# Gathering the first expert's tokens with the selection as the stationary operand

## The reference, cut to what matters

```python
def moe_swiglu(h, router, w1, w3, w2):
    logits = t @ router                       # t: 256 x 1024
    top_val, top_idx = lax.top_k(logits, 2)
    gates = softmax(top_val)
    # tokens of each expert are gathered in blocks, then for each block:
    #     y = (silu(xi @ w1[e]) * (xi @ w3[e])) @ w2[e]
    # w1, w3: 1024 x 3584, w2: 3584 x 1024 for each of 8 experts
    # and out[token] += y * gate
```

## Time and profile before

| | us |
|---|---|
| median of 3 runs | 1779.2 |
| lowest and highest | 1776.2 and 1781.97 |
| the profiled execution, its own time | 1776.49 |
| its span in the trace | 1774.6 |
| the gather on TensorE (L2348) | from 878.61, for 7.95 |
| item 0's first product (L2378) | 887.21 |

### The profile page before, as it was taken

How to read it: one execution, slowest core, us unless ns; L and a number is a source line. 1 busy time by engine, 2 the same in 40 slices (tenths; PEclk the granted TensorE clock), 3 DMA queues, 4 the chain that set the end, 5 groups by cost and what they waited for, 6 DMA issues and landing times.

```text
span 1774.6 us, 30337 instructions
## 1 busy us (share of the span) xinstructions
PE 1727.1 (97%) x13214; PEld 926.7 (52%) x13214; DVE 638.7 (36%) x1091; ACT 404.6 (23%) x796; POOL 202.2 (11%) x269
## 2 busy tenths in 40 slices
PE   7999989999999999999999999999999999999998
PEld 3787656878788888666833332333323233233433
DVE  2634586789855775362311001010110102001112
ACT  3523484422222223376100100001000010000010
POOL 1416332011101110433100000000000000000010
PEclk9999999999999999999999999999999999999999
DMA  9454500779664544133489999999999999999993
GB/s 357 145 189 170 151 1 3 258 264 322 206 221 143 190 137 168 48 131 118 157 331 418 416 393 419 396 414 417 388 419 398 410 417 391 418 403 407 417 421 161
DMA packets 136284, 498.40 MB, mean 281 GB/s; under 512 B 6849, under 2 KB 47425, under 8 KB 127969
## 3 DMA queue, kind: packets, MB, share of 16 engines
q1 hardware_dynamic: 132624, 489.58, 72.0%
q0 software_dynamic: 1920, 5.77, 1.1%
q10 hardware_dynamic: 1616, 1.22, 0.2%
HBM read 474.13 MB, written 22.41 MB: 280 GB/s over the span
## 4 chain that ended last, share of the span: by engine, by line
PE 84%; DMA 5%; DVE 5%; ACT 2%; POOL 2%; issue 1%; SPq 0%; ACTq 0%; DVEq 0%; POOLq 0%
PE ps L2378 31%; PE ps L2394 10%; PE ps L2197 6%; PE ps L2199 6%; PE ps L2198 6%; PE ps L2401 5%; DMA ring_up<-in_moe_w 4%; PE ps L2048 2%; PE ps L2069 2%; PE ps L1989 2%; PE ps L1990 2%; PE ps L1991 2%; PE ps L2143 2%; PE ps L2088 1%; PE ps L2112 1%; DMA ring<-in_ffn_w_up 1%
## 5 line engine op out<-in xcount | busy, mean ns | idle before, releaser
L2378 PE MATMUL ps<-ring_up,xg 128*32 128x448 f32 x3840 | 366.7, 539 | 3.4 <-DMA ring_up<-in_moe_w 3.4
L2378 PEld LDWEIGHTS ps<-ring_up,xg 128*32 128x32 f32 x3840 | 118.8, 110 | 246.0 <-issue 240.1
L2378 PE MATMUL ps<-ring,xg 128*32 128x448 f32 x2304 | 223.5, 542 | 0.7 <-DVE xg L1900 0.7
L1862 DVE TENSOR_TENSOR hid<-hid,ps 128x448 f32<-128x448 f32 x48 | 26.9, 617 | 531.8 <-PE ps L2378 531.8
L2378 PEld LDWEIGHTS ps<-ring,xg 128*32 128x32 f32 x2304 | 71.6, 110 | 147.3 <-issue 145.5
L2197 PE MATMUL ps<-hTh,fsa 128*128 128x512 f32 x328 | 128.7, 392 | 3.7 <-DVE fsb L1642 3.4
L2199 PE MATMUL ps<-hTl,fsa 128*128 128x512 f32 x328 | 128.1, 391 | 0.0
L2394 PE MATMUL ps<-ring_up,hidT 128*32 128x512 f32 x1024 | 121.3, 592 | 1.1 <-DMA ring_up<-in_moe_w 1.1
L1198 ACT ACTIVATE fsa<-ring 128x1024 fp32r<-128x1024 f32 (+2 forms) x73 | 68.8, 943 | 226.0 <-PE ps L2199 220.0
L1310 ACT ACTIVATE ytok<-ps 32x512 f32<-32x512 f32 x32 | 18.8, 589 | 412.5 <-PE ps L2401 412.3
L1361 DVE SCALAR_TENSOR_TENSOR scr<-ring,scond,scr 128x512 f32<-128x512 f32 x140 | 110.8, 826 | 1.1
(11 more groups left out here) (327 smaller groups left out, 2517.0 us busy)
## 6 DMA issues: line engine op xcount, KB each, us to landing
ring_up<-in_moe_w SPq DMA_DIRECT2D x80, 1792.0 KB, 19.8
ring<-in_moe_w SPq DMA_DIRECT2D x48, 1792.0 KB, 19.5
ring<-in_ada_w SPq DMA_DIRECT2D x24, 2048.0 KB, 8.3
ring<-in_moe_w SPq DMA_DIRECT2D x24, 2048.0 KB, 24.5
ring_up<-in_moe_w SPq DMA_DIRECT2D x24, 2048.0 KB, 24.2
ring_up<-in_moe_w SPq DMA_DIRECT2D x16, 1024.0 KB, 22.9
ring<-in_ev_w_in SPq DMA_DIRECT2D x6, 2048.0 KB, 10.5
ring<-in_ffn_w_gate SPq DMA_DIRECT2D x11, 1024.0 KB, 6.9
```

Of the source, the lines that this page charges most:

```text
L2378: ins = pe.matmul(ps[3 * z + t][32 * q:32 * q + 32, 0:FC], xg[:, k, 32 * t:32 * t + 32], w[:, c, FC * q:FC * (q + 1)], start=(k == 0), sto ...
```

## The change

In `gather_first` the operands change places. `sel` becomes stationary, 32 of the 96 token columns at a time, and `htok` moves, 256 neighbouring features at a time. The four quarters of the 1024 features go to the four column quarters of the array, so token j of quarter q ends at partition 32q + j. That is 3 token groups x 2 token tiles x 4 quarters = 24 products of 32 x 256. Each token group has its own PSUM bank (4, 5, 3), and `m_gat` counts three. The result isn't in `xg`'s layout: each 32 x 32 block has to be turned. VectorE does that with one transpose for each token group, from PSUM straight into `xg`, reading features with a step of 8. The transposes stand on VectorE directly behind the step that gives the number of items, and ahead of its register load. ScalarE's copy and VectorE's copy go away.

```diff
@@ ScalarE
-            act.wait_ge(m_gat, 1)
-            act.activation(xg[:, 0:4, :], v3(ps[4][:, 0:4 * CAP], CAP), ACT.Copy).then_inc(m_x, 1)
@@ VectorE
             dve.tensor_scalar(nit[:, 0:1], col[5][:, 1:2], float(NE - 1), None, ALU.add).then_inc(items_rd, 1)
+            for t in range(GT):
+                dve.wait_ge(m_gat, t + 1)
+                ins = dve.transpose(xg[:, :, 32 * t:32 * t + 32],
+                                    ps[(4, 5, 3)[t]][:, 0:256].rearrange("p (i c) -> p c i", c=KT))
+            ins.then_inc(m_x, 2)
             dve.wait_ge(items_rd, 1)
...
-            dve.wait_ge(m_gat, 2)
-            dve.tensor_copy(xg[:, 4:8, :], v3(ps[5][:, 0:4 * CAP], CAP)).then_inc(m_x, 1)
@@ TensorE, gather_first
-                for hh in range(2):
-                    for q in range(4):
-                        for t in range(2):
-                            rows = htok[:, t, :].rearrange("p (i c) -> p c i", c=KT)
-                            ins = pe.matmul(ps[4 + hh][:, q * CAP:(q + 1) * CAP], rows[:, 4 * hh + q, :],
-                                            sel[:, t, :], start=(t == 0), stop=(t == 1))
+                for t in range(GT):
+                    for h in range(2):
+                        for q in range(4):
+                            ins = pe.matmul(ps[(4, 5, 3)[t]][32 * q:32 * q + 32, 0:256],
+                                            sel[:, h, 32 * t:32 * t + 32], htok[:, h, 256 * q:256 * q + 256],
+                                            start=(h == 0), stop=(h == 1))
                     ins.then_inc(m_gat, 1)
```

## The result

The changed kernel takes 1769.1 us, the median of 17 runs (1764.4 to 1776.5), against 1777.0 for the kernel before in 17 runs alongside (1771.2 to 1784.9). The ratio is 0.995, with a 95% interval from 0.9938 to 0.9962, so the gain is between 6.8 and 11.0 us. The three runs of before that were shown had a median of 1779.2. With 17 runs it is 1777.0, so the starting point was 2.2 us too high and the gain about 3 us too small.

A forecast was written before the change was run, and what follows sets the result against it. TensorE was taken to pace most of the expert stage and the DMA stream its end. TensorE's gain of 4.5 + 1.35 = 5.8 us, capped at 5.0, gave 1779.2 - 5.0 = 1774.2 us, range 1769.5 to 1779.

The forecast's parts named there:

- the starting point: Time of the kernel before, from which the gain was subtracted: 1779.2 us, the median of three runs.
- the DMA stream: Weight transfers in the expert stage: can win only their idle time, 5.0 us, which caps TensorE's 5.8 us gain.
- the turning: Three VectorE transposes behind the gather, 0.66 us each, set its end; the first product comes 4.5 us earlier.
- the clock: Gather and start of item 0: the clock no longer falls to half, which gains 1.35 us in item 0.
- What bounds the kernel: Expert stage: TensorE sets the pace for most of it, the DMA stream at the end; 3.4 us of weight waits.
- The gather: Ahead of item 0: 48 pairs of 256 columns replace 32 pairs in 7.95 us, taking 2.62 us plus 0.16 tail.
- The 0.8 us of added late waits: Items 6 and 7: 0.8 us of TensorE's gain comes back as additional waiting for weights.
- (b): Rival, end of the expert stage: TensorE sets the end, so the whole 5.8 us count, 1773.4 us; chance 0.18.
- (a): Rival, gather and item 0: the clock falls all the same, gain 1.8 us, 1777.4, or 3 to 4.5; chance 0.20.
- (c): Rival, gather: the quarters' weight loads aren't hidden, 1778 us, or 1785.7 fully serial; chance 0.04 without and 0.03 with loss.

The follow-up runs named there:

- e3: The kernel before with the two 1024 KB units of each item loaded only to a quarter: 1770.8 us, ratio 0.9954.
- e5: The changed kernel with six more keep-busy TensorE products between the gather and item 0: 1777.0 us, ratio 0.999.
- e6: The changed kernel with six VectorE products ahead of the last transpose, so that TensorE idles: 1778.2 us, ratio 1.0003.
- e4: The changed kernel with the two 1024 KB units of each item loaded only to a quarter: 1765.4 us, ratio 0.9927.
- e7: The changed kernel with the gather products reordered so that four records in a row go to the same quarter: 1769.4 us, ratio 0.9948.
- e1: The kernel before, unchanged, with a second trace: 1778.5 us, ratio 1.0004.
- e10: The kernel before, unchanged, with a third trace: 1774.4 us, one run.

## Why the prediction was wrong

One step failed, the cap that the DMA stream was to put on the gain. The other mechanisms were the right ones, but two of their terms were too small: the turning and the clock. All three misses are in the gain and to the same side: 0.8 us by the cap, 0.65 by the turning and 0.85 by the clock. The starting point was off besides.

- **What bounds the kernel**: right. TensorE paces the expert stage until the weight stream has used up its lead, and e3 puts a price on the rest, 7 us in place of the 3.4 of the waits that I read. Those were the waits of L2378 alone; L2394 waited 1.3 us more for weights in the same trace.
- **The gather**: 2.80 us measured, 2.78 forecast. Scaling the item's product from 448 to 256 columns held within 1%.
- **The turning**: mis-sized. I took 0.66 us a transpose; two take 0.77 back to back and one alone 0.45. The nearest row by its step was the wrong guide; the floor from the transpose without a step (0.36) was close. With 0.66 VectorE sets the end. With 0.4 it waits for the last token group, and only one transpose lies behind the gather. The first product comes 5.1 us earlier, not 4.5.
- **The clock**: right in kind. It stays at 1.00, and e5 against e6 shows that what TensorE does before the item decides it. Its worth was read from the one trace at hand, 1.35 us. The four traces with the old gather lose 1.3 to 2.7, in the mean 2.3.
- **The DMA stream**: this step failed. I let it cap the gain at 5.0 us by adding up idle time from the DMA share. The bytes say 6.5 in the first pair of traces and 7.4 in the mean of three: after the gap a stretch with a share of 0.86 moved 276 GB/s, where item 1 with a share of 1.01 moved 408, and 0.86 of that would be some 350. Share is not rate. The stream did follow the first release of a slot, 6.36 us sooner against the gather's start, so it takes nothing from TensorE's gain. The 0.8 us of added late waits didn't come: late waits are 2.1 to 2.8 us in the three traces of the changed kernel and 2.7 to 6.2 in the three of the one before.
- **Rivals**: the time came out nearest to (b), with 5.8 to 6.7 us of gain, but not by its reason. TensorE does not set the end alone, as e3 and e4 show; the weight stream simply starts as much earlier as TensorE does. (a) was wrong (item 0 takes 108.2 us in all six traces with the early start) and (c) was wrong (e7).
- **The starting point**: three runs stood for a distribution with a spread of 14 us. Their median was 2.2 us high. From 1777.0 the same gain gives 1772.0, with a range of 1767.3 to 1776.8 around it, and the measured time lies in that. But the gain would have been as much too small.

The sum as the traces have it: 5.16 us of start (8.61 to 3.45) and 2.2 of clock (item 0 from a mean of 110.4 in three traces of before to 108.2) are 7.3 us, against 7.9 by the medians and an interval from 6.8 to 11.0. The clock on record for every run supports the second term: it is 6.0 us less clock time lost. Some 4 of these lie between the fall of the clock and item 0's first product, and cost nothing, since the old gather took 7.95 to 7.97 us however much of it ran at half clock. By this estimate some 2 us are left for item 0. What is left, 0.6 us by the medians and up to 1.6 by the ratio's middle, is within the scatter of the late waits. Whether the change shortens these by a microsecond or two can't be told from eleven traces, and stays open.

## What to carry to other kernels

Where a small product is bound by loading 128-column operands that have a step, swap the operands and put four quarters side by side: here 7.95 us became 2.80, and the layout was repaired by three transposes of 0.4 us of which only the last was exposed. When a stage is paced by a stream that is released by the first use of a buffer, a saving ahead of it moves the stream too; judge that by the bytes moved up to a given point, not by the share of busy DMA engines. And price a clock dip from several executions: it is worth different amounts in each, and time won at one dip can be lost at another. The mean granted clock of every run says what one trace can't.

## What the runs showed of the hardware

- A VectorE transpose of 128 x 256 from PSUM, read with a step of 8, took 0.39 us back to back (0.77 for two) and 0.45 alone; one of 128 x 384 from SBUF with the same step takes 0.866. The shorter form costs less than half, which neither proportion (0.58) nor the difference of two rows (0.74) told.
- Four records in a row to one column quarter ran as fast as neighbours in different quarters (2.85 against 2.80 us for 48).
- The old gather took the same time at both clocks: 7.95 us where its first 1.03 us were at full clock, 7.97 in e1 and e10, where all but the first 0.2 to 0.3 us were at half. That is 0.25 us a pair. Weight loads fill nearly all of it, as the first row below shows; the next two rows, from just before the gather, are pairs with 128 columns of weights that lie side by side and 8 that move, at 0.11 us a pair (0.22 from the start of one row to the next). So the loading of weights with a step of 8 sets the old gather's pace, and not the columns that move; that the step is what makes it slow is likely from these rows, but no run changed the step alone.

```profile
878.61 7.71 PEld L2348 LDWEIGHTS ps<-sel,etab 128*128 128x128 f32 x32 [1.47 <-DVE sel L1812]
```

```profile
876.42 0.37 PE L2337 MATMUL ps<-etab,ones 128*128 128x8 f32 x2
876.65 0.37 PE L2338 MATMUL ps<-etab,ones 128*128 128x8 f32 x2
```

- 1.6 of 44 MB less per item took away all waits for weights and most of the scatter between runs.
